# Gate matrices of a product-key expert layer: fp32 one-hot products against three bf16 products per token

## What is computed

```python
idx = e1 * N_KEYS + e2                      # 128 x 128 experts
gate = jax.nn.softmax(top_s, axis=-1)       # 8 heads x 16 chosen = 128 slots a token
act = jax.nn.gelu(jnp.einsum('tkd,td->tk', U[it], xt), approximate=False) * gt
return jnp.einsum('tk,tkd->td', act, V[it])
```

## Time and profile before

| | us |
|---|---|
| median of 3 runs | 3432.32 (3430.85 to 3433.84) |
| the profiled execution, its own time | 3429.56 |
| its span, first to last instruction | 3427.8 |
| PE busy | 3230.4 (94%) |
| DVE busy | 1994.8 (58%) |
| ACT busy | 1229.1 (36%) |
| DMA engines, mean busy share on the main queue | 48.4% |
| TensorE clock granted, mean | 0.978 of full speed |

### The profile page before, as it was taken

The page is one execution under the profiler, slowest core; times in us unless marked ns, Lnnn a source line. Parts: engine busy times, 40 slices in busy tenths (PEclk is TensorE's granted clock), DMA queues, the critical chain, the costliest instruction groups (busy, mean ns, idle before and its releaser), DMA issues.

```text
span 3427.8 us, 46395 instructions
## 1 busy us (share of the span) xinstructions
PE 3230.4 (94%) x18908; PEld 2759.3 (80%) x18908; DVE 1994.8 (58%) x3248; ACT 1229.1 (36%) x1873; POOL 20.0 (1%) x41
## 2 busy tenths in 40 slices
PE   7997889999999999999999997997689999999998
PEld 3664478888888888888888885896689999999997
DVE  3347335998565655344444444336838988756665
ACT  2413233333333333333333333325235444444443
POOL 0000000000000000000000000000000000000000
PEclk9999999999999999999999998998799999999999
DMA  5420223555666665765565551321046777788884
GB/s 198 173 85 1 74 80 97 147 146 162 215 234 214 238 234 157 263 195 192 192 192 189 193 182 65 111 70 60 0 160 192 208 244 241 236 280 261 266 268 142
DMA packets 232412, 587.82 MB, mean 171 GB/s; under 512 B 20791, under 2 KB 103816, under 8 KB 228552
## 3 DMA queue, kind: packets, MB, share of 16 engines
q1 hardware_dynamic: 227088, 528.57, 48.4%
q0 software_dynamic: 4208, 53.27, 4.0%
q10 hardware_dynamic: 904, 3.01, 0.3%
HBM read 483.06 MB, written 101.71 MB: 171 GB/s over the span
## 4 chain that ended last, share of the span: by engine, by line
PE 75%; DVE 15%; ACT 5%; issue 3%; DMA 1%; POOL 0%; ACTq 0%; DVEq 0%; SPq 0%; POOLq 0%
PE ps L532 31%; PE ps L846 22%; PE ps L723 10%; PE ps L798 5%; DVE w_lo L1634 5%; ACT w_hi L1144 3%; PE ps L759 2%; PE ps L577 1%; DVE arena L1659 1%; PE ps L608 1%; DVE arena L1551 1%; DVE arena L1545 1%; PE ps L601 1%; PE ps L778 1%; DVE arena L1793 0%
## 5 line engine op out<-in xcount | busy, mean ns | idle before, releaser
L1634 DVE TENSOR_TENSOR w_lo<-wring,w_hi 128x1024 fp32r<-128x1024 f32 x512 | 626.5, 1224 | 685.2 <-ACT w_hi L1144 683.2
L532 PE MATMUL ps<-a_hi,w_hi 128*128 128x512 f32 (+1 forms) x2048 | 700.5, 342 | 9.4 <-DVE w_lo L1634 5.5
L846 PE MATMUL ps<-act_hi,w_hi 128*128 128x512 f32 (+1 forms) x2048 | 697.8, 341 | 5.7 <-DVE act_lo L1665 5.7
L532 PE MATMUL ps<-a_hi,w_lo 128*128 128x512 f32 (+1 forms) x2048 | 689.0, 336 | 0.0
L846 PE MATMUL ps<-act_lo,w_hi 128*128 128x512 f32 (+1 forms) x2048 | 688.4, 336 | 0.0
L532 PE MATMUL ps<-a_lo_q,w_hi 128*128 128x512 f32 (+1 forms) x2048 | 688.1, 336 | 0.0
L846 PE MATMUL ps<-act_hi,w_lo 128*128 128x512 f32 (+1 forms) x2048 | 687.9, 336 | 0.0
L1144 ACT CAST w_hi<-wring 128x1024 fp32r<-128x1024 f32 x512 | 533.7, 1043 | 227.1 <-PE ps L846 227.1
L532 PEld LDWEIGHTS ps<-a_hi,w_hi 128*128 128x128 f32 x2048 | 388.4, 190 | 61.8 <-issue 11.5
L846 PEld LDWEIGHTS ps<-act_hi,w_hi 128*128 128x128 f32 x2048 | 388.0, 189 | 52.9 <-issue 6.2
L532 PEld LDWEIGHTS ps<-a_hi,w_lo 128*128 128x128 f32 x2048 | 388.3, 190 | 41.6
(11 more groups left out here) (245 smaller groups left out, 3387.8 us busy)
## 6 DMA issues: line engine op xcount, KB each, us to landing
wring<-in_u SPq DMA_DIRECT2D x256, 512.0 KB, 4.1
wring<-in_v SPq DMA_DIRECT2D x256, 512.0 KB, 4.3
gates<-arena POOLq DMA_DIRECT2D x24, 2048.0 KB, 9.1
acts<-arena SPq DMA_DIRECT2D x128, 256.0 KB, 4.6
arena<-acts SPq DMA_DIRECT2D x128, 256.0 KB, 3.4
arena<-gates SPq DMA_DIRECT2D x16, 2048.0 KB, 11.6
late_ring<-in_ada SPq DMA_DIRECT2D x28, 1024.0 KB, 6.3
wring<-in_ada SPq DMA_DIRECT2D x40, 512.0 KB, 6.1
```

Of the source, the lines that this page charges most:

```text
L532: ins = pe.matmul(o, l, r, start=n == 0, stop=n == len(pairs) - 1, **kw)
L846: ins = pe.matmul(value_sum(l, c), w, x, start=m == 0 and n == 0 and (l == 0 or c % 2 == 0), stop=m == NKEY - 1 and n == 2, skip_group_che ...
L1634: tt(WLO[:, k % 4].rearrange("p k n -> p (k n)"), wring[:, n % RING * TILE:(n % RING + 1) * TILE], WHI[:, k % 4].rearrange("p k n -> p (k ...
```

## The change

The one-hots and the gated part become bf16, and the gate is cut into three bf16 parts (`GHI`, `GMID`, `GLO`), whose sum stands for the fp32 gate. Each token's matrix is then three products, accumulated in PSUM, of the same `OHB` by each of three gated one-hots. The layout of `EQK`, `OHB` and `OHA` is now pairs of tokens innermost, so that an operand of one token is read with a step of two bf16 elements. `KEYNUM` shrinks from 8 copies of each number to 2. The parts and the bf16 copies of both keys are made before the first oct of each 128 tokens.

```diff
-        OHB = view(22528, "p (b u e) -> p b u e", b=2, u=OCT, e=P)
-        OHA = view(24576, "p (b u e) -> p b u e", b=2, u=OCT, e=NKEY)
-        EQK = over("first_onehot", 32768, 2 * NKEY * OCT, BF16)[:, :].rearrange("p (b e u) -> p b e u", b=2, u=OCT)
-        KEYNUM = over("key_numbers", 33792, P * OCT, BF16)[:, :].rearrange("p (e u) -> p e u", u=OCT)
+        EQK = over("first_onehot", 32768, 2 * NKEY * OCT, BF16)[:, :].rearrange("p (b v e w) -> p b v e w", b=2, v=OCT // 2,
+                                                                               w=2)
+        KEYNUM = over("key_numbers", 33792, P * 2, BF16)[:, :].rearrange("p (e w) -> p e w", w=2)
+        OHB = over("second_onehot", 22528, 2 * P * OCT, BF16)[:, :].rearrange("p (b v e w) -> p b v e w", b=2, v=OCT // 2, w=2)
+        OHA = over("gated_onehot", 23552, 6 * NKEY * OCT, BF16)[:, :].rearrange("p (b x v e w) -> p b x v e w", b=2, x=3,
+                                                                               v=OCT // 2, w=2)
...
-                        ins = pe.matmul(ps[:, 2 + h, u * NKEY:(u + 1) * NKEY], OHB[:, n % 2, 4 * h + u, :],
-                                        OHA[:, n % 2, 4 * h + u, :], start=True, stop=True)
+                        for x in range(3):
+                            ins = pe.matmul(ps[:, 2 + h, u * NKEY:(u + 1) * NKEY], OHB[:, n % 2, 2 * h + u // 2, :, u % 2],
+                                            OHA[:, n % 2, x, 2 * h + u // 2, :, u % 2], start=x == 0, stop=x == 2)
...
-                    step.done(dve.tensor_copy(KEY1[:, i * P:(i + 1) * P], SL[:, 1, i * P:(i + 1) * P]))
+                    t = slice(i * P, (i + 1) * P)
+                    dve.tensor_copy(KEY1[:, t], SL[:, 1, t])
+                    dve.tensor_copy(KEY2[:, t], SL[:, 2, t])
+
+                    step.done(dve.tensor_copy(GHI[:, t], SL[:, 0, t]))
+                    step.done(tt(GREST, SL[:, 0, t], GHI[:, t], ALU.subtract))
+                    step.done(dve.tensor_copy(GMID[:, t], GREST))
+                    step.done(tt(GLO[:, t], GREST, GMID[:, t], ALU.subtract))
...
-                tt(EQK[:, n % 2], KEYNUM, KEY1[:, toks].unsqueeze(1).to_broadcast([P, NKEY, OCT]), ALU.is_equal)\
-                    .then_inc(S["eq_ready"], 1)
+                def spread(x):
+                    return x[:, toks].rearrange("p (v w) -> p v w", w=2).unsqueeze(2).to_broadcast([P, OCT // 2, NKEY, 2])
+
+                numbers = KEYNUM.unsqueeze(1).to_broadcast([P, OCT // 2, NKEY, 2])
+                tt(EQK[:, n % 2], numbers, spread(KEY1), ALU.is_equal).then_inc(S["eq_ready"], 1)
                 wait(dve, S["oh_used"], 2 * (o - 1))
-                tt(OHB[:, n % 2], iota[:, :].unsqueeze(1).to_broadcast(shape),
-                   SL[:, 2, toks].unsqueeze(2).to_broadcast(shape), ALU.is_equal)
+                tt(OHB[:, n % 2], numbers, spread(KEY2), ALU.is_equal)
                 yield
                 dve.wait_ge(S["eq_ready"], o + 1)
-                tt(OHA[:, n % 2], EQK[:, n % 2].rearrange("p e u -> p u e"),
-                   SL[:, 0, toks].unsqueeze(2).to_broadcast(shape), ALU.mult).then_inc(S["oh_ready"], 1)
+                for x, part in enumerate((GHI, GMID, GLO)):
+                    ins = tt(OHA[:, n % 2, x], EQK[:, n % 2], spread(part), ALU.mult)
+                ins.then_inc(S["oh_ready"], 1)
```

More of the change, by code:

```diff
@@ L285, in build @@
                     for n, at in (("w_hi", 14336), ("w_lo", 18432))]
-        OHB = view(22528, "p (b u e) -> p b u e", b=2, u=OCT, e=P)
-        OHA = view(24576, "p (b u e) -> p b u e", b=2, u=OCT, e=NKEY)
         ACH, ACL = [over(n, at, ZRING * T)[:, :].rearrange("p (r t) -> p r t", r=ZRING)
                     for n, at in (("act_hi", 22528), ("act_lo", 24576))]
-        EQK = over("first_onehot", 32768, 2 * NKEY * OCT, BF16)[:, :].rearrange("p (b e u) -> p b e u", b=2, u=OCT)
-        KEYNUM = over("key_numbers", 33792, P * OCT, BF16)[:, :].rearrange("p (e u) -> p e u", u=OCT)
+        EQK = over("first_onehot", 32768, 2 * NKEY * OCT, BF16)[:, :].rearrange("p (b v e w) -> p b v e w", b=2, v=OCT // 2,
[4 more added lines that the diff above has]
+                                                                               v=OCT // 2, w=2)
         KEY1 = over("slot_keys", 34304, T, BF16)[:, :]
+        KEY2, GHI, GMID, GLO = [over(n, at, T, BF16)[:, :] for n, at in
+                                (("slot_keys2", 12288), ("gate_hi", 12544), ("gate_mid", 12800), ("gate_lo", 13056))]
+        GREST = arena[:, 13312:13312 + P]
         I16 = iota[:, 0:TOPK]
@@ L1603, in key_numbers @@
             def key_numbers():
-                step.done(dve.tensor_copy(KEYNUM, iota[:, :].unsqueeze(2).to_broadcast([P, P, OCT])))
+                step.done(dve.tensor_copy(KEYNUM, iota[:, :].unsqueeze(2).to_broadcast([P, P, 2])))
             def onehots(l, n):
@@ L1610, in onehots @@
                     dve.wait_ge(S["slots_in"], l * TT + i + 1)
-                    step.done(dve.tensor_copy(KEY1[:, i * P:(i + 1) * P], SL[:, 1, i * P:(i + 1) * P]))
+                    t = slice(i * P, (i + 1) * P)
[5 more added lines that the diff above has]
+                    step.done(tt(GLO[:, t], GREST, GMID[:, t], ALU.subtract))
                 toks = slice(n * OCT, (n + 1) * OCT)
-                shape = [P, OCT, NKEY]
-                tt(EQK[:, n % 2], KEYNUM, KEY1[:, toks].unsqueeze(1).to_broadcast([P, NKEY, OCT]), ALU.is_equal)\
-                    .then_inc(S["eq_ready"], 1)
+                def spread(x):
+                    return x[:, toks].rearrange("p (v w) -> p v w", w=2).unsqueeze(2).to_broadcast([P, OCT // 2, NKEY, 2])
+                numbers = KEYNUM.unsqueeze(1).to_broadcast([P, OCT // 2, NKEY, 2])
+                tt(EQK[:, n % 2], numbers, spread(KEY1), ALU.is_equal).then_inc(S["eq_ready"], 1)
                 wait(dve, S["oh_used"], 2 * (o - 1))
-                tt(OHB[:, n % 2], iota[:, :].unsqueeze(1).to_broadcast(shape),
-                   SL[:, 2, toks].unsqueeze(2).to_broadcast(shape), ALU.is_equal)
+                tt(OHB[:, n % 2], numbers, spread(KEY2), ALU.is_equal)
                 yield
                 dve.wait_ge(S["eq_ready"], o + 1)
-                tt(OHA[:, n % 2], EQK[:, n % 2].rearrange("p e u -> p u e"),
-                   SL[:, 0, toks].unsqueeze(2).to_broadcast(shape), ALU.mult).then_inc(S["oh_ready"], 1)
+                for x, part in enumerate((GHI, GMID, GLO)):
+                    ins = tt(OHA[:, n % 2, x], EQK[:, n % 2], spread(part), ALU.mult)
+                ins.then_inc(S["oh_ready"], 1)
                 yield
```

## The result

| | us |
|---|---|
| before, median of 4 runs | 3431.7 (3430.85 to 3433.84) |
| after, median of 4 runs | 3396.53 (3395.76 to 3398.41) |
| ratio, 95% interval | 0.9897 (0.988 to 0.9915) |
| after, span of the profiled execution | 3394.2 |

What follows compares the result with a forecast made beforehand. PE alone was taken to bound both gate stages, with DVE hidden. From the profiled 3429.6 us, 96 shorter octs took 17.7, DVE and the rest 0, giving 3411.9; the median's 2.8 offset made it 3414.6 us, range 3386 to 3455.

Steps and rivals of the forecast that it cites:

- t = 66.8: PE's octs: ns from one 128-column bf16 product to the next, loads hidden; 24 make 1.603 us, 96 octs give -17.7 us.
- the lower end: PE's octs: a bf16 product every 57.5 ns, 53.3 of stream plus 4; oct 1.380 us, -39 us.
- The fixed piece: PE's octs: time a product takes beyond its column stream, put at 13.5 ns as in one-pass fp32r products.
- its ends at 61 and 113: PE's weight loads in the octs: one every 61 ns if fast, every 113 ns if as slow as fp32.
- The first rival: PE's octs: bf16 load fast but not wholly hidden, 81 ns a product, +15 us, 3447 us; chance 0.21.
- The second: PE's load path in 96 octs: bf16 weights load as slowly as fp32, +89 us, 3521 us; chance 0.15.
- the 81 ns: PE's octs: the skill's figure for a sustained load and 128-column product; oct 1.944 us, an estimated +15 us.
- The last rival: PE's octs: chip skips repeated loads of the same `OHB`, 57.5 ns a product, 3393 us; included in the forecast's 0.56.
- I let the change of type cost nothing.: PE between octs and neighbouring products: switching type was priced at 0; a longer first product afterwards would break the sum.
- as priced by `EQK`: DVE's five new bf16 operations: 0.69 us each, like the existing all-bf16 one; DVE stays hidden, 0 us.
- the bound I kept for it: DVE's five new operations: between 0.69 and 2.0 us each; the one-element case at 1.23 gave 3436 us, chance 0.05.
- The heads of 128 tokens: DVE's six small operations per 128 tokens, six times, some 1.3 us more each time; priced 0, at most +8 us.

## Why the prediction was wrong

The measured time lies inside the range (3386 to 3455), but the gain is twice the forecast one. The mechanism was right: PE alone bounds both stages, the oct's length is the gain, DVE stays hidden. **The step that failed is a term of the sum that was mis-sized: "I take t = 66.8, the value of the one-pass product, which is the nearest row in form".** The measured t is 58.3 ns over a whole oct and 57.5 inside it, the lower end. With it the oct takes 1.40 us, and 96 x (1.787 - 1.40) = 37 us. That the end was met so exactly is luck: it was 53.3 and 4 ns from the two-pass rows, and the runs show 53.3, 2.5 and 1.7 for the step of two, to which the prediction gave nothing.

- *The fixed piece.* I carried the 13.5 ns of an fp32r product over to bf16 because both are one instruction and one pass. The run with 256 columns shows that it belongs to fp32r: at equal length bf16 pays 2.5 ns and fp32r 13.5. The fp32 rows in the same group had shown 4 for a product of two passes; the number of passes was the wrong likeness. What makes the 13.5 in fp32r is open.
- *The load.* I left its ends at 61 and 113 and took it to hide. It does, with more room than any row said: a pair of load and product came every 25 ns with 32 columns. The first rival (load not hidden whole) falls by this. The second (bf16 weights at 113 ns) falls by the pace of 57.5 itself, and the run with 120 columns shows that even a bf16 load outside its fast mode hides behind 128 columns. With the first falls the 81 ns that the Trainium skill gives for such a pair ("TensorE: Matmul & The Clock Gate", section "Back-to-back issue gap"): 96 streams of 24 such pairs went at 58.3 ns here, and the sum by that figure would have had the wrong sign.
- *The last rival*, that loads of the same `OHB` are skipped, gave nearly the right time for a wrong reason. There are 2304 loads for 2304 products, and the third part costs as much as the others.
- *"I let the change of type cost nothing."* It costs where fp32r products follow at once: the stretch behind an oct is 0.08 us longer in the 8 plain turns of layer 0 and 0.05 in the 32 octs of layer 1. An oct of layer 1 so gains 1.79 - 1.39 - 0.05 = 0.35 us, as read (7.54 to 7.19). Behind the 56 octs that the modulation group follows it is 0.01. In all that is 2 to 3 us (37.2 - 34.9). The two errors had opposite signs, and the small one hid a little of the large one. Most of it is the first fp32r load, which a short stream does not cover: one more change costs 7.6 us, and the distance over the seam stays 0.34 to 0.35 us whether 32, 128 or 256 columns stream before it. The run in fp32r shows a loss with no change of type, so the length of the stream ahead counts, and "change of type" is not the whole name for it.
- *A step of two on PE* was also priced at nothing. It costs 1.7 ns a product, 0.04 us an oct, some 4 us in all.
- *DVE.* Each of the five operations lasts 0.68 to 0.69 us, as priced by `EQK`. The run with keys innermost shows that the bound I kept for it was real: at 1.22 us layer 1 turns over to DVE.
- *The heads of 128 tokens* cost nothing, as said; layer 1's stage still starts and runs on PE.

The forecast's distance to the result is 18 us. The term of t is 96 x 24 x (66.8 - 58.3) ns = 19.6 us of it, less the 2.3 lost behind the octs; what is left is 1 us, no more than single executions differ by.

## What to carry to other kernels

Where small products load new weights each time, ask for both the stream and the load which is longer. Going to bf16 took away both fp32 costs at once, the second pass and the slow load, so three bf16 products (3 x 58 ns) beat one fp32 product (2 x 112 ns) even though they load three times. Look also at the load of what stands behind: a short last stream leaves part of the first fp32r load in the open. In these runs it paid to keep the small products together, and a longer last stream lost less. On DVE, an input that repeats pairs of bf16 elements ran at 0.69 us for 1024 elements, and one that repeats a single element at 1.22.

If the gate need not be kept to full precision, two shorter versions were measured: two bf16 parts, 3349.7 us, and one fp32r product, 3339.5 us. Each rounds the gate more than the changed kernel does.

## What the runs showed of the hardware that was not expected

- Load rows of weights in the gate stages: 192 ns for 128 columns of fp32 or fp32r, 133 for 120 of bf16, 97 for 128 of bf16. Eight columns fewer make a bf16 load longer. (The 140 ns of fp32 transposes in the earlier trace rows is not explained by this.)
- The loads of 97 ns do not run ahead of an fp32r stream: the first of an oct starts with its own product, at 1300.82, and the second product comes 70 ns later. With 120 columns the first load starts at 1300.88, with the last fp32r product ahead (1300.87), and the second product comes after 58 ns. The two kernels take the same time.
- The pair of load and product goes down to 25 ns at 32 columns (0.61 us for 24).
- An fp32r product pays 13.5 ns beside a stream of 256 or 512 columns, a bf16 product 2.5 beside 128 or 256 with its streamed operand at a step of one.
- Reading both operands at a step of two bf16 elements costs PE 1.7 ns a product (57.5 against 55.8 by starts, 1.40 against 1.36 us for 24).
